# First loads of a one-core decoder step: norm's vector joined to x, one x block issued by ScalarE, the first weight half rounded in two pieces

## The chip, the cores and the metric

The kernel runs on one core of one Trainium2 chip. The metric is the device time of one execution in microseconds (us), as the median of several runs. Engines are named as the profile names them: PE (TensorE matmul), PEld (its weight load), DVE (VectorE), ACT (ScalarE), POOL (GpSimd), SP (SyncE, which here only issues transfers). A name with a q behind it (SPq, ACTq) is the sequencer of that engine, where issuing a transfer takes its time.

## What is computed

One layer of a decoder trunk for 256 prompt tokens and 8 times 4 sample tokens, 288 in all, with a model width of 2048:

```python
xn = rmsnorm(x, norm_mix_g)
proj = jnp.einsum('bld,de->ble', xn, w_in)            # 2048 -> 4096, eight strips of 512
a_val, a_gate, p, c_h, c_b, c_c, d_u, d_v = jnp.split(proj, N_PROJ, axis=-1)
...                                                   # four token mixers A, B, C, D
x = x + jnp.einsum('ble,ed->bld', mix, w_out)
...
xn = rmsnorm(x, norm_ffn_g)
h = jax.nn.silu(jnp.einsum('bld,df->blf', xn, w_gate)) * jnp.einsum('bld,df->blf', xn, w_up)
x = x + jnp.einsum('blf,fd->bld', h, w_down)          # d_ff = 5632
```

A last rmsnorm closes it. All is float32. For this change only the first line and the first strip of the second matter: x times norm's vector `norm_mix_g`, as the moving operand of the products with `w_in`. The factor of the root of the mean square is applied behind the product.

## The kernel before

**Layout.** x lies transposed in `x_sb`: 128 partitions are 128 of the 2048 model columns, and 16 blocks (`KD`) of 288 columns (`T`, the tokens) stand side by side. `X[:, b, :]` is block b. The vectors of the norms and mixers lie in `vec`, with `norm_mix_g` in its first 16 columns (`v(name, b)` is one column).

**Products in three parts.** Every float32 product is made from three products of rounded operands. ScalarE rounds a weight tile `raw` to `wh` (high part), VectorE makes `wl` = `raw` - `wh` (low part); x is treated the same way to `xh_sb` and `xl_sb`, with norm's vector as the scale of the conversion. PE adds wh*xh, wh*xl and wl*xh in the same bank.

**Tiles.** A weight tile is two blocks of 128 rows by 512 columns, 512 KB, in a ring of 4 slots. PE meets 4 column groups of 128 per block, so 12 products of 128x288 per block and 24 per tile. The first two tiles (`HALF_TILES`) are loaded, rounded and used in halves of one block each, by `load_half`, `hi_half`, `lo_half` and `by_kind`; tiles 2 to 5 go whole but still by kind (all 8 wh*xh products, then 8 wh*xl, then 8 wl*xh), and from tile 6 on `products` does the three kinds for each column group in turn.

**Order of the work.** It is written out by hand for each engine; semaphores order the engines among each other. At the start SP issues, one behind the other, x block 0, half 0 of tile 0, x block 1, half 1 of tile 0, x blocks 2 and 3, the two halves of tile 1, x blocks 4 and 5, tile 2 and so on (L364 to L377). From tile 4 on it waits for a slot of the ring. ScalarE issues the first 16 columns of `vec` itself (L458), loads its function table, and then converts and rounds in the order of the tiles: block 0, half 0, block 1, half 1, blocks 2 and 3, the halves of tile 1, blocks 4 and 5, tile 2. VectorE follows it. PE first runs 9 warm-up products (`WARM`, L1247) on a constant, then `by_kind`, whose three groups wait for the x block and the weight half, for the low part of x, and for the low part of the half. The semaphores at the start are `vec_landed`, `x0_landed` (block 0), `first_landed[0]` (half 0 of tile 0), `x_landed[0]` (block 1), `raw_landed[0]` (half 1), and `first_hi`, `first_lo`, `hi_ready`, `lo_ready`, `x_hi`, `x_lo` for what is rounded.

Of the kernel before, what the change touches and what calls it, by code (L numbers as in the profile page):

```python
# [26 lines left out]
P = 128  # L27
D = 2048
KD = D // P
# [3 lines left out]
GRP = 512  # L33
# [57 lines left out]

VECS = [("norm_mix_g", KD), ("conv_a_b", NG), ("ln_a_g", NG), ("ln_a_b", NG), ("pool_scale", NG),
        ("sgu_ln_g", NG), ("sgu_ln_b", NG), ("out_norm_g", KD), ("norm_ffn_g", KD), ("final_norm_g", KD),
# [54 lines left out]
def hybrid_step(nc, a, o):  # L148
    ctx = ExitStack()
    with ctx:  # L150
        def sb(name, cols, dt=F32):
            return ctx.enter_context(nc.sbuf_tensor(name, [P, cols], dt))
# [4 lines left out]
        def blocks(t, n=NG):  # L157
            return t.rearrange("p (n t) -> p n t", n=n)


        x_sb = sb("x_sb", KD * T)
        xh_sb, xl_sb = sb("xh_sb", KD * T, F32R), sb("xl_sb", KD * T, F32R)
        mh_sb, ml_sb = sb("mh_sb", KD * T, F32R), sb("ml_sb", KD * T, F32R)
        raw = sb("raw", RING * TILE)
        wh, wl = sb("wh", RING * TILE, F32R), sb("wl", RING * TILE, F32R)
        X = blocks(x_sb[:, :], KD)
        XH, XL = blocks(xh_sb[:, :], KD), blocks(xl_sb[:, :], KD)
# [41 lines left out]
        def v(name, b):  # L209
            return vec[:, VROW[name] + b:VROW[name] + b + 1]  # L210

        def tap(k, b):
# [45 lines left out]
        def gained(bs):  # L258

            return T0[:, bs.start - 3 * NG:bs.stop - 3 * NG, :] if bs.start >= 3 * NG else GAINED[:, bs, :]  # L260

        Y = x_sb[:, :].rearrange("p (h b t) -> p h b t", h=2, b=KD)
        TOKENS = [slice(h * HT, h * HT + HT) for h in range(2)]
# [6 lines left out]
        x_landed = [sem(f"x_landed{i}") for i in range(XQ)]  # L270
        vec_landed, sgu_landed, mats_landed, hist_landed = (sem(n) for n in (
            "vec_landed", "sgu_landed", "mats_landed", "hist_landed"))
        first_landed = [sem(f"first_landed{t}") for t in range(HALF_TILES)]
# [80 lines left out]
        def _(sp):  # L354
# [8 lines left out]

            sp.dma_start(X[:, 0:1, :], a["x"][:, 0:1, :]).then_inc(x0_landed, 16)  # L364
            load_half(0, 0, first_landed[0])
            sp.dma_start(X[:, 1:2, :], a["x"][:, 1:2, :]).then_inc(x_landed[0], 16)
            load_half(0, 1, raw_landed[0])

            for t in range(1, T_LOOP):
                if t < XQ:  # L370
                    bs = slice(t * TK, (t + 1) * TK)
                    sp.dma_start(X[:, bs, :], a["x"][:, bs, :]).then_inc(x_landed[t], 16)
                if t < HALF_TILES:
                    load_half(t, 0, first_landed[t])
                    load_half(t, 1, raw_landed[t])
                else:
                    load(t, tile_source(t), t - RING + 1 if t >= RING else None, t % RING)  # L377
                if t == XQ:
                    sp.dma_start(vec[:, KD:], a["vec"][:, KD:]).then_inc(hist_landed, 16)
                if t == XQ + 1:  # L380
                    for buf, width, name in ((G, GA, "hist_a"), (PP, PA, "hist_p"), (C, CA, "hist_c")):
                        sp.dma_start(buf[:, :, width:], a[name]).then_inc(hist_landed, 16)
                if t == XQ + 2:
                    sp.dma_start(WT, a["sgu_wt"]).then_inc(sgu_landed, 16)
                if t == XQ + 3:
                    sp.dma_start(PWV, a["pool_w"].rearrange("g c d -> c g d")).then_inc(mats_landed, 16)
                    sp.dma_start(brow[:, :], a["sgu_rows"].to_broadcast([P, NG * P + NG * NS * NS])).then_inc(mats_landed, 16)
# [68 lines left out]
        def _(act):  # L456
            chain = Chain(act, act_chain)
            act.dma_start(vec[:, 0:KD], a["vec"][:, 0:KD]).then_inc(vec_landed, 16)  # L458

# [39 lines left out]
            def x_block(b):  # L499
                act.activation(XH[:, b, :], X[:, b, :], ACT.Copy, scale=v("norm_mix_g", b)).then_inc(x_hi, 1)  # L500

# [5 lines left out]
            def hi_half(t, k):  # L507
                act.wait_ge(*((first_landed[t], 16) if k == 0 else (raw_landed[t], 16)))
                half = slice(k * GRP, (k + 1) * GRP)
                act.activation(slot(wh, t)[:, half], slot(raw, t)[:, half], ACT.Copy).then_inc(first_hi if k == 0 else hi_ready, 1)  # L510

            act.wait_ge(const_ready, 1)
            table(ACT.Copy)
            act.wait_ge(vec_landed, 16)
            act.wait_ge(x0_landed, 16)
            x_block(0)
            hi_half(0, 0)
            act.wait_ge(x_landed[0], 16)
# [177 lines left out]
        def _(dve):  # L696
# [22 lines left out]
            def x_block(b):  # L719
                dve.wait_ge(x_hi, b + 1)  # L720
                dve.scalar_tensor_tensor(out=XL[:, b, :], in0=X[:, b, :], scalar=v("norm_mix_g", b),
                                         in1=XH[:, b, :].bitcast(F32), op0=ALU.mult, op1=ALU.subtract).then_inc(x_lo, 1)
# [131 lines left out]

            dve.wait_ge(vec_landed, 16)
            x_block(0)
# [336 lines left out]
        def _(pe):  # L1193
# [57 lines left out]
            def by_kind(t, ks, hi_made, lo_made):  # L1251
# [3 lines left out]
                pe.wait_ge(x_hi, last_x)  # L1255
                pe.wait_ge(*hi_made)
                for k in ks:
                    for n in range(NG):
                        pe.matmul(bank[n][:, 0:T], W_H[:, k, n * P:(n + 1) * P], XH[:, t * TK + k, :], start=(t == 0 and k == 0), stop=False)  # L1259
                pe.wait_ge(x_lo, last_x)  # L1260
# [155 lines left out]
```

## Time and profile before

| what | value |
|---|---|
| median of three runs | 1177.95 us (1177.62 to 1178.06) |
| the profiled execution's own time | 1178.1 us |
| its span in the trace | 1176.4 us |
| PE busy | 1164.3 us (99%), 8718 products |
| DVE busy | 763.0 us (65%) |
| ACT busy | 502.1 us (43%) |
| POOL busy | 17.6 us (1%) |
| read from memory | 193.00 MB |
| engines of DMA queue q1 (issued by SP) | 54.4% of 16 engines' span |

The span runs from the first instruction to the last of one execution; 1.7 us of the execution lie outside it. Busy times of the engines overlap, and PE's share says which of them has no room. A view by stretches tells where PE is not busy, the timeline of one engine tells what its idle time waited for (in brackets: idle us, and what ended it), and the chain that ended last follows the program back from its end, at each step to what released it.

### The profile page before, as it was taken

Reading aid. Unit: us, or ns where it says so; the run is one execution under the profiler, and the core shown is the slowest. Engines: PE = TensorE matmul, PEld = TensorE weight load, DVE = VectorE, ACT = ScalarE, POOL = GpSimd, SP = SyncE. Lnnn points to the kernel's source line nnn. Section 1 sums busy time; section 2 is a strip of 40 time slices with the busy share of each in tenths; the row PEclk is TensorE's granted clock in tenths of the full one; section 3 lists DMA queues with packets and bytes.
Section 4 is the critical chain, followed back from the end, with each engine's and each line's share of the span. In section 5 each row is a group of like instructions: output and inputs, shape, how many; then the busy total and the mean of one; then the engine's idle time right before and its main releaser. Section 6 shows DMA issues by size and latency. Waiting matters only on the chain.

```text
span 1176.4 us, 22033 instructions
## 1 busy us (share of the span) xinstructions
PE 1164.3 (99%) x8718; PEld 1163.1 (99%) x8718; DVE 763.0 (65%) x1154; ACT 502.1 (43%) x623; POOL 17.6 (1%) x52
## 2 busy tenths in 40 slices
PE   9999999999999999999999999999999999999996
PEld 9999999999999999999999999999999999999996
DVE  6799999987775644744646456455565465645655
ACT  8544545446643333333333343333333333333345
POOL 0000010000000000000000000000000000000003
PEclk9999999999999999999999999999999999999998
DMA  9665545555455555545555555555554555555542
GB/s 313 227 181 171 157 149 170 164 175 161 151 175 172 158 172 161 162 145 191 162 160 163 164 169 164 160 161 165 170 164 143 180 161 170 165 162 161 163 156 84
DMA packets 105385, 197.08 MB, mean 168 GB/s; under 512 B 7936, under 2 KB 11136, under 8 KB 105344
## 3 DMA queue, kind: packets, MB, share of 16 engines
q1 hardware_dynamic: 103088, 195.38, 54.4%
q10 hardware_dynamic: 2256, 1.14, 0.3%
q8 instruction: 28, 0.46, 0.2%
q14 instruction: 13, 0.11, 0.0%
HBM read 193.00 MB, written 3.49 MB: 167 GB/s over the span
## 4 chain that ended last, share of the span: by engine, by line
PE 98%; DVE 0%; DMA 0%; issue 0%; ACT 0%; SPq 0%; DVEq 0%
PE bank L1229 32%; PE bank L1231 32%; PE bank L1230 32%; DMA x_sb<-in_x 0%; PE bank L1259 0%; PE bank L1263 0%; PE bank L1267 0%; DVE x_sb L1176 0%; PE bank L1316 0%; PE bank L1207 0%; ACT xh_sb L500 0%; PE bank L1215 0%; DVEq L150 0%; SPq L362 0%; DVE s_bc L1168 0%
## 5 line engine op out<-in xcount | busy, mean ns | idle before, releaser
L702 DVE TENSOR_TENSOR wl<-raw,wh 128x1024 fp32r<-128x1024 f32 x358 | 435.5, 1222 | 356.1 <-ACT wh L464 355.5
L464 ACT ACTIVATE wh<-raw 128x1024 fp32r<-128x1024 f32 x358 | 379.0, 1061 | 601.0 <-PE bank L1231 595.5
L1229 PE MATMUL bank<-xh_sb,wh 128*128 128x288 f32 x1872 | 554.3, 296 | 0.0
L1230 PE MATMUL bank<-xl_sb,wh 128*128 128x288 f32 x1872 | 552.2, 295 | 0.0
L1231 PE MATMUL bank<-xh_sb,wl 128*128 128x288 f32 x1872 | 550.4, 294 | 0.0
L1231 PEld LDWEIGHTS bank<-xh_sb,wl 128*128 128x128 f32 x1872 | 352.6, 188 | 0.0
L1230 PEld LDWEIGHTS bank<-xl_sb,wh 128*128 128x128 f32 x1872 | 351.5, 188 | 0.0
L1229 PEld LDWEIGHTS bank<-xh_sb,wh 128*128 128x128 f32 x1872 | 350.8, 187 | 0.0
L1229 PE MATMUL bank<-mh_sb,wh 128*128 128x288 f32 x960 | 284.2, 296 | 0.0
L1230 PE MATMUL bank<-ml_sb,wh 128*128 128x288 f32 x960 | 283.2, 295 | 0.0
L1231 PE MATMUL bank<-mh_sb,wl 128*128 128x288 f32 x960 | 282.3, 294 | 0.0
L1231 PEld LDWEIGHTS bank<-mh_sb,wl 128*128 128x128 f32 x960 | 180.8, 188 | 0.0
L1230 PEld LDWEIGHTS bank<-ml_sb,wh 128*128 128x128 f32 x960 | 180.2, 188 | 0.0
L1229 PEld LDWEIGHTS bank<-mh_sb,wh 128*128 128x128 f32 x960 | 179.9, 187 | 0.2 <-issue 0.2
L835 DVE TENSOR_TENSOR x_sb<-bank,x_sb 128x288 f32<-128x288 f32 x207 | 82.0, 448 | 14.7 <-PE bank L1231 14.7
L787 DVE SCALAR_TENSOR_TENSOR work<-g_sb,vec,work 128x256 f32<-128x256 f32 x120 | 52.3, 485 | 0.1
L839 DVE TENSOR_TENSOR p_sb<-bank,g_sb 128x288 f32<-128x288 f32 x44 | 18.9, 453 | 20.2 <-PE bank L1231 20.2
L649 ACT ACTIVATE mh_sb<-p_sb 128x288 fp32r<-128x288 f32 x44 | 18.7, 447 | 17.4 <-DVE p_sb L839 17.4
L843 DVE TENSOR_TENSOR ml_sb<-p_sb,mh_sb 128x288 fp32r<-128x288 f32 x44 | 19.0, 454 | 3.3
L849 DVE TENSOR_TENSOR g_sb<-g_sb,work 128x288 f32<-128x288 f32 x44 | 17.1, 450 | 0.0
L852 DVE TENSOR_TENSOR g_sb<-g_sb,s_bc 128x288 f32<-128x288 f32 x44 | 17.1, 448 | 0.0
L448 POOL TENSOR_TENSOR vt<-work 128x288 f32<-128x288 f32 x1 | 1.2, 1177 | 993.6 <-ACT work L667 993.6
(176 smaller groups left out, 350.3 us busy)
## 6 DMA issues: line engine op xcount, KB each, us to landing
raw<-in_w_gate SPq DMA_DIRECT2D x88, 512.0 KB, 3.7
raw<-in_w_up SPq DMA_DIRECT2D x88, 512.0 KB, 3.6
raw<-in_w_down SPq DMA_DIRECT2D x88, 512.0 KB, 3.8
raw<-in_w_in SPq DMA_DIRECT2D x62, 512.0 KB, 4.3
raw<-in_w_out SPq DMA_DIRECT2D x32, 512.0 KB, 4.0
x_sb<-in_x SPq DMA_DIRECT2D x7, 288.0 KB, 7.2
out_y<-x_sb SPq DMA_DIRECT2D x7, 288.0 KB, 2.2
raw<-in_w_in SPq DMA_DIRECT2D x4, 256.0 KB, 5.0
```

Source lines behind the costliest of these rows:

```text
L464: act.activation(slot(wh, t), slot(raw, t), ACT.Copy).then_inc(hi_ready, 1)
L649: act.activation(MH[:, b, :], HU[:, b, :], ACT.Copy).then_inc(h_hi, 1)
L702: dve.tensor_tensor(slot(wl, t), slot(raw, t), slot(wh, t).bitcast(F32), ALU.subtract).then_inc(lo_ready, 1)
L787: dve.scalar_tensor_tensor(out=acc, in0=src, scalar=tap(k, b), in1=acc, op0=ALU.mult, op1=ALU.add).then_inc(conv_done, 1)
L835: dve.tensor_tensor(X[:, b, :], src[:, 0:T], X[:, b, :], ALU.add).then_inc(banks_free, 1)
L839: dve.tensor_tensor(HU[:, n, :], src[:, 0:T], SG[:, n, :], ALU.mult).then_inc(banks_free, 1)
L843: dve.tensor_tensor(ML[:, b, :], HU[:, b, :], MH[:, b, :].bitcast(F32), ALU.subtract).then_inc(h_lo, 1)
L849: dve.tensor_tensor(SG[:, n, :], SG[:, n, :], T0[:, n, :], ALU.mult).then_inc(ffn_silu, 1)
L852: dve.tensor_tensor(SG[:, n, :], SG[:, n, :], s_bc[:, :], ALU.mult).then_inc(ffn_scaled, 1)
L1229: pe.matmul(banks[n][:, 0:T], W_H[:, k, cols], hi_, start=(first and k == 0), stop=False)
L1230: pe.matmul(banks[n][:, 0:T], W_H[:, k, cols], lo_, start=False, stop=False)
L1231: mm = pe.matmul(banks[n][:, 0:T], W_L[:, k, cols], hi_, start=False, stop=(last and k == TK - 1))
```

## The change

Norm's vector no longer lies in `vec` but in 16 columns in front of x, in memory and in the core (`gx_sb`; `x_sb` is its part behind them). The first transfer brings these 16 columns together with block 0, and the transfer that ScalarE issued for them is gone, with its semaphore `vec_landed`. The transfer of block 1 leaves SP's queue; ScalarE issues it behind its conversion of block 0. The first half of tile 0 is rounded by ScalarE in two pieces of 256 columns, `leading_hi` and `first_hi`; PE waits for the first piece ahead of its first product and for the second ahead of its third.

```diff
-VECS = [("norm_mix_g", KD), ("conv_a_b", NG), ("ln_a_g", NG), ("ln_a_b", NG), ("pool_scale", NG),
+VECS = [("conv_a_b", NG), ("ln_a_g", NG), ("ln_a_b", NG), ("pool_scale", NG),
...
-        x_sb = sb("x_sb", KD * T)
+        gx_sb = sb("x_sb", KD + KD * T)
+        x_sb = gx_sb[:, KD:]
...
+        def mix_gain(b):
+            return gx_sb[:, b:b + 1]
...
-            sp.dma_start(X[:, 0:1, :], a["x"][:, 0:1, :]).then_inc(x0_landed, 16)
+            sp.dma_start(gx_sb[:, 0:KD + T], a["x"][:, 0:KD + T]).then_inc(x0_landed, 16)
             load_half(0, 0, first_landed[0])
-            sp.dma_start(X[:, 1:2, :], a["x"][:, 1:2, :]).then_inc(x_landed[0], 16)
             load_half(0, 1, raw_landed[0])
...
-                    sp.dma_start(vec[:, KD:], a["vec"][:, KD:]).then_inc(hist_landed, 16)
+                    sp.dma_start(vec[:, :], a["vec"]).then_inc(hist_landed, 16)
...
-            act.dma_start(vec[:, 0:KD], a["vec"][:, 0:KD]).then_inc(vec_landed, 16)
...
+            def hi_first_half():
+                act.wait_ge(first_landed[0], 16)
+                for cols, made in ((slice(0, GRP // 2), leading_hi), (slice(GRP // 2, GRP), first_hi)):
+                    act.activation(slot(wh, 0)[:, cols], slot(raw, 0)[:, cols], ACT.Copy).then_inc(made, 1)
+
             act.wait_ge(const_ready, 1)
             table(ACT.Copy)
-            act.wait_ge(vec_landed, 16)
             act.wait_ge(x0_landed, 16)
             x_block(0)
-            hi_half(0, 0)
+            act.dma_start(gx_sb[:, KD + T:KD + 2 * T], a["x"][:, KD + T:KD + 2 * T]).then_inc(x_landed[0], 16)
+            hi_first_half()
...
-                pe.wait_ge(*hi_made)
+                if t == 0 and ks[0] == 0:
+                    pe.wait_ge(leading_hi, 1)
+                else:
+                    pe.wait_ge(*hi_made)
                 for k in ks:
                     for n in range(NG):
+                        if t == 0 and k == 0 and n == NG // 2:
+                            pe.wait_ge(*hi_made)
```

SP's queue at the start of the program, before. `x_sb<-in_x 128x288` is one x block, `128x576` are two, `raw<-in_w_in 128x512` is a weight half:

```order
L364 DMA x_sb<-in_x 128x288
L362 DMA raw<-in_w_in 128x512
L366 DMA x_sb<-in_x 128x288
L362 DMA raw<-in_w_in 128x512
L372 DMA x_sb<-in_x 128x576
L362 DMA raw<-in_w_in 128x512 x2
```

And after, where `128x304` is norm's vector with block 0:

```order
L368 DMA x_sb<-in_x 128x304
L366 DMA raw<-in_w_in 128x512 x2
L375 DMA x_sb<-in_x 128x576
L366 DMA raw<-in_w_in 128x512 x2
L375 DMA x_sb<-in_x 128x576
```

The transfer of block 1 has left the queue between the two halves of tile 0, and everything behind it stands one place further ahead.

ScalarE at the start, before. `xh_sb<-x_sb,vec` is the conversion of an x block, `wh<-raw` the rounding of weights:

```order
L458 DMA vec<-in_vec 128x16
L496 ACT_TABLE_LOAD
L496 ACTIVATE scrap<-ones_d 128x1 [waits const_ready]
L500 ACTIVATE xh_sb<-x_sb,vec 128x288 [waits x0_landed,vec_landed]
L510 ACTIVATE wh<-raw 128x512 [waits first_landed0]
L500 ACTIVATE xh_sb<-x_sb,vec 128x288 [waits x_landed0]
L510 ACTIVATE wh<-raw 128x512 [waits raw_landed0]
```

And after:

```order
L498 ACT_TABLE_LOAD
L498 ACTIVATE scrap<-ones_d 128x1 [waits const_ready]
L502 ACTIVATE xh_sb<-x_sb 128x288 [waits x0_landed]
L523 DMA x_sb<-in_x 128x288
L517 ACTIVATE wh<-raw 128x256 [waits first_landed0]
L517 ACTIVATE wh<-raw 128x256
L502 ACTIVATE xh_sb<-x_sb 128x288 [waits x_landed0]
L512 ACTIVATE wh<-raw 128x512 [waits raw_landed0]
```

A transfer has gone from the head of the queue, another has come between the first conversion and the first rounding, and that rounding is now two instructions.

## Rows read from the trace of the kernel before

**Rows 1.** Stretches: length, busy (count) of five engines, granted clock, DMA share, GB/s.

```profile
5.00:10.00 5.00, 3.72 (x27) 3.31 (x25) 2.92 (x6) 2.82 (x6) 0.00 (x0) 1.00 0.93 304
10.00:14.00 4.00, 4.00 (x30) 4.00 (x31) 3.19 (x6) 3.38 (x7) 0.00 (x0) 1.00 1.05 404
14.00:1165.00 1151.00, 1150.81 (x8636) 1150.41 (x8635) 749.07 (x1129) 489.88 (x599) 15.45 (x20) 1.00 0.55 166
1165.00:1176.40 11.40, 1.79 (x12) 1.56 (x12) 7.22 (x16) 3.33 (x9) 0.00 (x0) 0.67 0.55 208
```

**Rows 2.** Timeline of PE: start, us, engine, line, operation, tiles, count, idle before.

```profile
1.07 4.06 PE L1248 MATMUL bank<-ones_d 128*128 128x128 f32 x18 [1.07 <-POOL ones_d L408]
5.04 0.76 PE L1259 MATMUL bank<-xh_sb,wh 128*128 128x288 f32 x4
...
7.25 0.77 PE L1259 MATMUL bank<-xh_sb,wh 128*128 128x288 f32 x4 [0.40 <-ACT wh L510]
...
9.97 0.77 PE L1259 MATMUL bank<-xh_sb,wh 128*128 128x288 f32 x4 [0.89 <-ACT wh L510]
...
13.23 1.22 PE L1259 MATMUL bank<-xh_sb,wh 128*128 128x288 f32 x8
```

**Rows 3.** Chain that ended last, in order of time: start, us, what.

```profile
2.69 5.63 DMA x_sb<-in_x
8.32 0.02 issue
8.35 0.96 ACT xh_sb L500 x2
9.31 0.53 ACT wh L510
9.84 0.14 issue
```

**Rows 4.** Two transfers by line: x block 0, and tile 1's first half.

```profile
L364 SPq DMA_DIRECT2D x_sb<-in_x x1: 402/402/402, 0.8 to 0.8; - x1
...
DMA to landing us min/median/max: 2.2/2.2/2.2
...
L362 SPq DMA_DIRECT2D raw<-in_w_in x1: 431/431/431, 3.2 to 3.2; - x1
...
DMA to landing us min/median/max: 5.8/5.8/5.8
```

**Rows 5.** Timeline of ScalarE.

```profile
3.24 0.53 ACT L500 ACTIVATE xh_sb<-x_sb,vec 128x288 fp32r<-128x288 f32 x1 [0.47 <-DMA vec<-in_vec]
4.27 0.63 ACT L510 ACTIVATE wh<-raw 128x512 fp32r<-128x512 f32 x1 [0.49 <-DMA raw<-in_w_in]
5.83 0.54 ACT L500 ACTIVATE xh_sb<-x_sb,vec 128x288 fp32r<-128x288 f32 x1 [0.94 <-DMA x_sb<-in_x]
6.48 0.63 ACT L510 ACTIVATE wh<-raw 128x512 fp32r<-128x512 f32 x1
...
11.73 1.06 ACT L464 ACTIVATE wh<-raw 128x1024 fp32r<-128x1024 f32 x1 [0.37 <-DMA raw<-in_w_in]
```

**Rows 6.** Timeline of ScalarE and its sequencer at 61 us.

```profile
61.65 1.06 ACT L464 ACTIVATE wh<-raw 128x1024 fp32r<-128x1024 f32 x1 [2.14 <-PE bank L1231]
61.73 0.64 ACTq L564 DMA_DIRECT2D out_a<-g_sb  x1
```

**Rows 7.** Timeline of SP's sequencer.

```profile
1.74 0.42 SPq L366 DMA_DIRECT2D x_sb<-in_x  x1
...
3.16 0.92 SPq L362 DMA_DIRECT2D raw<-in_w_in  x2
```

**Rows 8.** Stretches of one microsecond each, as in rows 1.

```profile
3.00:4.00 1.00, 1.00 (x7) 1.00 (x6) 0.11 (x1) 0.53 (x1) 0.06 (x2) 1.00 0.85 193
...
5.00:6.00 1.00, 1.00 (x9) 0.99 (x8) 0.62 (x1) 0.17 (x1) 0.00 (x0) 1.00 0.81 235
```

More of the change, by code:

```diff
@@ L165, in hybrid_step @@
         wh, wl = sb("wh", RING * TILE, F32R), sb("wl", RING * TILE, F32R)
-        X = blocks(x_sb[:, :], KD)
+        X = blocks(x_sb, KD)
         XH, XL = blocks(xh_sb[:, :], KD), blocks(xl_sb[:, :], KD)
@@ L260, in gained @@
             return T0[:, bs.start - 3 * NG:bs.stop - 3 * NG, :] if bs.start >= 3 * NG else GAINED[:, bs, :]
-        Y = x_sb[:, :].rearrange("p (h b t) -> p h b t", h=2, b=KD)
+        Y = x_sb.rearrange("p (h b t) -> p h b t", h=2, b=KD)
         TOKENS = [slice(h * HT, h * HT + HT) for h in range(2)]
@@ L270, in hybrid_step @@
         x_landed = [sem(f"x_landed{i}") for i in range(XQ)]
-        vec_landed, sgu_landed, mats_landed, hist_landed = (sem(n) for n in (
-            "vec_landed", "sgu_landed", "mats_landed", "hist_landed"))
+        sgu_landed, mats_landed, hist_landed = (sem(n) for n in ("sgu_landed", "mats_landed", "hist_landed"))
+        leading_hi = sem("leading_hi")
         first_landed = [sem(f"first_landed{t}") for t in range(HALF_TILES)]
@@ L370, in _ @@
                 if t < XQ:
-                    bs = slice(t * TK, (t + 1) * TK)
-                    sp.dma_start(X[:, bs, :], a["x"][:, bs, :]).then_inc(x_landed[t], 16)
+                    at = slice(KD + t * TK * T, KD + (t + 1) * TK * T)
+                    sp.dma_start(gx_sb[:, at], a["x"][:, at]).then_inc(x_landed[t], 16)
                 if t < HALF_TILES:
@@ L499, in x_block @@
             def x_block(b):
-                act.activation(XH[:, b, :], X[:, b, :], ACT.Copy, scale=v("norm_mix_g", b)).then_inc(x_hi, 1)
+                act.activation(XH[:, b, :], X[:, b, :], ACT.Copy, scale=mix_gain(b)).then_inc(x_hi, 1)
             def x_part(q):
@@ L720, in x_block @@
                 dve.wait_ge(x_hi, b + 1)
-                dve.scalar_tensor_tensor(out=XL[:, b, :], in0=X[:, b, :], scalar=v("norm_mix_g", b),
+                dve.scalar_tensor_tensor(out=XL[:, b, :], in0=X[:, b, :], scalar=mix_gain(b),
                                          in1=XH[:, b, :].bitcast(F32), op0=ALU.mult, op1=ALU.subtract).then_inc(x_lo, 1)
@@ L852, in silu @@
                     dve.tensor_tensor(SG[:, n, :], SG[:, n, :], s_bc[:, :], ALU.mult).then_inc(ffn_scaled, 1)
-            dve.wait_ge(vec_landed, 16)
+            dve.wait_ge(x0_landed, 16)
             x_block(0)
@@ L1378 @@
     host = {
-        "x": tokens.reshape(T, KD, P).transpose(2, 1, 0),
+        "x": np.concatenate([rows("norm_mix_g"), tokens.reshape(T, KD, P).transpose(2, 1, 0).reshape(P, KD * T)], axis=1),
         "vec": np.concatenate([rows(name) for name, _ in VECS], axis=1),
```

## The prediction, made before the changed kernel had run

> **What bounds the kernel now.** I read the stretches first, because a change that touches only the first loads can gain only what the first stretch loses. From 14 us to 1165 us the profile has TensorE (PE) busy 1150.81 of 1151.00 us, and 4.00 of 4.00 between 10 and 14 us, at a granted clock of 1.00, the 2.4 GHz level; behind 1165 us stands the closing norm with its stores, 11.40 us, which the change leaves alone [rows 1]. So the end of the program is the start of PE's unbroken run plus a fixed sum, and the reader should look for where that run starts. PE's own timeline gives it: nine warm-up products reach to 5.13 us, the first 12 real products start at 5.04 with no idle time before them, then come 0.40 us of waiting to 7.25 and 0.89 us to 9.97, both for ScalarE's rounding of a weight half (L510); from 9.97 on nothing waits [rows 2]. The chain that ended last says what 9.97 hangs on: the transfer of x blocks 2 and 3, issued at 2.69 and landing at 8.32, two x conversions to 9.31, the weight half 0.53 more to 9.84, and 0.14 of hand-over [rows 3]. That is the only path on which this change can move the end.
>
> **A ceiling comes before any sum.** All that PE idles between its first real product and its unbroken run is 0.40 + 0.89 = 1.29 us [rows 2]. The first product cannot start much before 5.0, since the warm-up holds PE until then. Even with every wait gone the gain is about 1.3 us, 0.11% of 1178 us. A measurement of this kernel tells about 0.2% (2.4 us) from no change, so a measurable gain is out of reach; the question is only which tenth of a microsecond it is, and whether something breaks.
>
> **Part 1, norm's vector in front of x.** It removes ScalarE's own transfer of vec and the wait for it. x block 0 was issued at 0.81 and took 2.2 us to land, so it was there at 3.0 [rows 4]; the first conversion started at 3.24, released by vec [rows 5]. The merged transfer carries 304 columns for 288, 6% more, so 3.0 to 3.05: the first conversion moves forward by about 0.2 us. What is late next is the first weight half: ScalarE idles 0.49 us for it up to 4.27 [rows 5]. The 0.2 us only lengthen that wait. Value 0. If the merged piece landed 0.5 us later, 3.55 + 0.53 = 4.08 would still be ahead of 4.27, so 0 on that side too.
>
> **Part 2, the first weight half rounded in two pieces.** A rounding of 512 columns takes 0.63 us and one of 1024 takes 1.06 [rows 5], so about 0.43 us per 512 columns and 0.2 fixed: a piece of 256 costs 0.40, the pair 0.7 to 0.8 against 0.63. The first piece is ready at 4.27 + 0.40 = 4.67, the second at 4.98 to 5.07. Before, the whole half was ready at 4.90. PE does not take the first piece at 4.67, because its warm-up holds it to about 5.0, where the real products start back to back with it [rows 2]. The products of columns 2 and 3 need the second piece 0.26 us after the first product, at 5.3, and get it by 5.1. So +0.05 us of gain at most and no loss at the start; and since PE then waits for block 1 and its weight half anyway (the 0.40 us to 7.25), it is swallowed. VectorE's subtraction of this half starts 0.1 to 0.2 us later, ahead of its use after eight products. Value 0.
>
> **Part 3, block 1 moved from SP's queue to ScalarE's.** Three things hang on it.
> First, ScalarE's own time. Its queue issues the transfer behind the first conversion. In this trace an issue on that queue began at 61.73, 0.08 us after an ACTIVATE of 1.06 us had started [rows 6], so the two overlap: the issue runs from about 3.1 to 3.7. Were it not to overlap, 3.03 + 0.53 + 0.64 = 4.20 is still before 4.27. Value 0 either way.
> Second, block 1 is issued at 3.1 for 1.74 before. The lower bound of its flight is the 2.2 us of a transfer into empty queues [rows 4], so 5.3; the upper one the 5.63 us that blocks 2 and 3 took in SP's queue [rows 3], so 8.7; between them stands its own old flight, 1.74 to 5.83, 4.1 us [rows 5, 7], so 7.2. I take 6.0 to 6.5, near the lower end, since ScalarE's queue holds nothing else while SP's holds four transfers. What it may cost: ScalarE needs 0.54 + 0.63 us and a gap of 0.11, 1.28 from 5.83 to 7.11 [rows 5], and is then free for blocks 2 and 3, which are awaited to 8.32. Block 1 may land as late as 8.32 - 1.28 = 7.04 before it delays them. At 6.5 PE's first wait grows by 0.6 us, and its second shrinks by as much. Value 0 at 6.5, and at 8.7 a loss of 1.7.
> Third, all that SP issues behind it comes 0.47 us earlier (the spacing from 2.69 to 3.16 [rows 3, 7]): blocks 2 and 3 at 2.21, tile 1's halves, blocks 4 and 5, tile 2. If flight times stay, all land 0.47 earlier. If the 16 DMA engines are what paces them, they land when they did, because the bytes up to there are the same with block 1 in them. The rows stand between. From 3 to 4 us the engines are busy 0.85 of the time at 193 GB/s, from 5 to 6 0.81 at 235 [rows 8], against 1.05 at 404 from 10 to 14 [rows 1]: not full, but near it. I take half of it, 0.25 us.
>
> A rule stands against this part. The Trainium skill ("DMA: Bandwidth & Descriptors", section "Issuing engines are not separate DMA queues") says that transfers started from several engines run on the same 16 DMA engines and interleave, and that this saves only issue time. By it the sum would be 0 instead of 0.25; it is the first rival.
>
> **What caps the gain behind it.** With blocks 2 and 3 early, the next things are late. Tile 1's first half, issued at 3.16 and 5.8 us in flight, lands at 8.96 [rows 4, 7]; with 0.53 and 0.14 behind it PE could start at 9.65, 0.32 earlier, if it does not move. Tile 2 landed at 11.73, where ScalarE waited 0.37 us for it, and is rounded at 12.79 [rows 5]; PE takes it up at 13.23 [rows 2], which leaves 0.3 us after a hand-over of 0.14. These two say that 0.3 is the limit unless the whole stream comes forward, and 0.25 lies under it.
>
> **Sum.** 0 + 0 + 0 + 0.25 = 0.25 us off. Against the profiled execution: 1178.1 - 0.25 = 1177.85. That execution lies 0.15 us over the median, so the time to be expected as a median is 1177.95 - 0.25 = 1177.7. The vec transfer that SP issues later keeps its 208 columns and its place; x_sb grows by 16 columns and vec shrinks by 16, and no steady instruction changes shape.
>
> **Rivals.**
> No movement: the engines pace the early stream, blocks 2 and 3 land at 8.32 as before. For it speaks that the old flights grow along the queue (2.2, 4.1, 5.63, 5.8 us); against it the unfilled 15 to 19% between 3 and 6 us. Time 1177.95. Chance 0.27.
> The stream comes forward whole: the 0.47 us carry through to tile 2, and PE's run starts at 9.5: 1177.95 - 0.47 = 1177.5, and 1176.65 if all 1.29 us went. Against it: ScalarE is free for blocks 2 and 3 only from about 7.1, and then needs 0.96 + 0.53 + 0.14, so 8.7 is the floor. Chance 0.15.
> Slower, by one mechanism: block 1 comes late on its new queue. The mechanism decides at a landing of 7.04; every 0.1 us past that costs 0.1, because conversion, rounding and blocks 2 and 3 stand behind it on ScalarE. With the old flight of 4.1 us it lands at 7.2 and costs 0.2; with 5.63 it costs 1.7, 1179.6. I price it at 0.5: 1178.45. Chance 0.12.
> Slower rows: with 16 columns in front, each partition's row of x starts elsewhere in memory, and its reads may be less efficient. If the x rows went at the 304 GB/s of 5 to 10 us where they could have 404 [rows 1], a transfer of 288 KB would take 0.97 us for 0.73, and two such lie ahead of 8.32: up to 0.48 us, 1178.4. Against it: nothing in the rows says that the start of a row matters. Chance 0.04.
> The Trainium skill ("DMA: Bandwidth & Descriptors", "How a descriptor splits into AXI transactions") says that a read that does not start on a 256-byte boundary fetches unused bytes; the new rows start 64 bytes on, which would make some beats per row more and a loss of under 0.1 us. No run shows it so far.
> The forecast itself (a gain between 0.1 and 0.4 us) has 0.42.
>
> **How the numbers follow.** Likeliest 1177.7. The three runs of before spread over 1177.62 to 1178.06, so 0.2 either way comes on top of each case. The range reaches from the stream that comes forward whole (1177.5 less 0.4) to the late block 1 at its price: 1177.1 to 1178.45. Faster by over 0.2% would need 2.4 us, above the ceiling of 1.29: 0.01. Slower by over 0.2% needs block 1 to land at 9.4, above the upper bound of 8.7: 0.02. Within 0.2%: 0.97.
>
> **What would show it.** Right: the last transfer on the chain is still an early one, PE's run starts between 9.6 and 9.9, the first conversion at about 3.05, the first real product still at 5.0, the issue on ScalarE's queue over before 4.2, block 1 there by 7.0. Part 2 is wrong if the first product starts before 4.9 or PE waits between its columns 1 and 2. Part 3 is wrong if the first wait of PE grows past 7.9. All of it is wrong if PE idles anywhere behind 10 us, or if the steady products change their pace: of the 8636 between 14 and 1165 us [rows 1] one nanosecond each is 8.6 us.

## The result, and the profile after

The changed kernel takes 1181.79 us (median of seven executions, 1179.21 to 1182.99), against 1177.63 us (1177.45 to 1178.06) for the kernel before, measured beside it: a ratio of 1.0033, with a 95% interval of 1.0024 to 1.0043. It is 4.2 us slower. The range had ended at 1178.45, and the chance given to a loss of over 0.2% was 0.02.

The profiled execution is the mildest of the seven, 1179.21 us, with a span of 1177.5 us against 1176.4. It shows the first part of the loss whole. PE's timeline (start, us, engine, line, operation, tiles, count, idle time before), to be held against [rows 2]:

```profile
4.89 0.78 PE L1271 MATMUL bank<-xh_sb,wh 128*128 128x288 f32 x4
...
6.03 0.69 PE L1279 MATMUL bank<-xh_sb,wl 128*128 128x288 f32 x4
9.41 0.78 PE L1271 MATMUL bank<-xh_sb,wh 128*128 128x288 f32 x4 [2.69 <-ACT wh L512]
...
14.27 1.22 PE L1271 MATMUL bank<-xh_sb,wh 128*128 128x288 f32 x8
```

The first group starts 0.15 us earlier, and then PE waits 2.69 us where it had waited 0.40. The second wait (0.89 us) is gone. The last row is the first product of tile 2, which stood at 13.23 [rows 2]. It is the best single reading of this case: from there on PE never stops, so its shift of 1.04 us is the shift of the end (1177.5 for 1176.4, 1.1 us). ScalarE's timeline and its sequencer, against [rows 5], say why:

```profile
3.10 0.54 ACT L502 ACTIVATE xh_sb<-x_sb 128x288 fp32r<-128x288 f32 x1 [0.80 <-DMA x_sb<-in_x]
3.10 0.42 ACTq L523 DMA_DIRECT2D x_sb<-in_x  x1
...
4.12 0.72 ACT L517 ACTIVATE wh<-raw 128x256 fp32r<-128x256 f32 x2 [0.48 <-DMA raw<-in_w_in]
...
8.21 0.54 ACT L502 ACTIVATE xh_sb<-x_sb 128x288 fp32r<-128x288 f32 x1 [3.37 <-DMA x_sb<-in_x]
8.65 0.61 ACT L512 ACTIVATE wh<-raw 128x512 fp32r<-128x512 f32 x1
```

The small edits came out as worked: the first conversion at 3.10, the issue of block 1 overlapping it and over at 3.52, the two pieces taking 0.72 us. Then ScalarE sits idle 3.37 us for block 1. The view of its line gives the flight, the time from the start of the issue to the landing:

```profile
L523 ACTq DMA_DIRECT2D x_sb<-in_x x1: 424/424/424, 3.1 to 3.1; - x1
...
DMA to landing us min/median/max: 5.1/5.1/5.1
```

The chain that ended last now names this transfer, where it had named the one of blocks 2 and 3 [rows 3]:

```profile
3.10 5.08 DMA x_sb<-in_x
8.19 0.02 issue
8.21 0.54 ACT xh_sb L502
8.74 0.53 ACT wh L512
9.27 0.14 issue
```

From 9.41 on PE is the chain itself. So far that is 1.1 us. The other six executions took 1181.47 us and more. What they have besides stands in the first experiment.

### The profile page after: what moved, and what is told of

It reads as the page before. It is cut to its first block, busy times and chain, and to the rows that moved or that the text cites. A ratio compares the mean times of both kernels' runs of the same rounds, so it can differ in the third digit from the quotient of the medians.

```text
span 1177.5 us, 22032 instructions
## 1 busy us (share of the span) xinstructions
PE 1163.9 (99%) x8718; PEld 1163.1 (99%) x8718; DVE 762.8 (65%) x1154; ACT 501.9 (43%) x624; POOL 18.5 (2%) x52
## 4 chain that ended last, share of the span: by engine, by line
PE 98%; DMA 1%; DVE 0%; issue 0%; ACT 0%; DVEq 0%
PE bank L1236 32%; PE bank L1238 32%; PE bank L1237 32%; DMA x_sb<-in_x 1%; PE bank L1271 1%; PE bank L1275 0%; PE bank L1279 0%; DVE x_sb L1183 0%; PE bank L1328 0%; PE bank L1214 0%; PE bank L1222 0%; DVEq L150 0%; DVE s_bc L1175 0%; ACT xh_sb L502 0%; PE bank L1308 0%
```

## The experiments

The theory behind them (one): block 1, issued late, lands behind what has been issued before it, whichever queue it is on, and PE's long wait for it then takes the granted clock down. Its rivals: the shifted x rows load slower; ScalarE's queue is slow in itself; the pieces of the first half do harm. "Theory two" in an expectation is the rival that this experiment sets against theory one, and not always the same. All medians stand beside the kernel before on the same chip.

**The changed kernel again** (no edit).

> The changed kernel again, for more executions of it. Theory one (block 1 lands late from ScalarE's queue, PE idles about 2.7 us, and in most executions the granted clock falls in or behind that gap): again about 1181.8 as a median against 1177.6, with a spread of some 2 us, and a profile that has either the 2.69 us wait at clock 1.00 (time near 1179.2) or the same or a longer wait and a stretch at half clock (time 1181 to 1183). Theory two (x rows that start 64 bytes on load slower): the same median, but then the wait would be for all x transfers, with their flights longer than before.

Measured 1181.68 us (1180.79 to 1182.23) against 1177.66, ratio 1.0032 (1.0020 to 1.0044). This time the profiled execution (1181.76 us, span 1180.0) is a typical one. PE's timeline:

```profile
10.44 0.77 PE L1271 MATMUL bank<-xh_sb,wh 128*128 128x288 f32 x4 [3.72 <-ACT wh L512]
...
12.45 1.16 PE L1271 MATMUL bank<-xh_sb,wh 128*128 128x288 f32 x4
13.41 1.16 PE L1275 MATMUL bank<-xl_sb,wh 128*128 128x288 f32 x4
...
16.83 1.22 PE L1271 MATMUL bank<-xh_sb,wh 128*128 128x288 f32 x8
```

and the stretches (length, busy and count of PE, PEld, DVE, ACT, POOL, granted clock, DMA share, GB/s):

```profile
10.00:11.00 1.00, 0.56 (x4) 0.59 (x5) 1.00 (x3) 1.00 (x3) 0.00 (x0) 1.00 1.04 402
11.00:12.00 1.00, 1.00 (x9) 1.00 (x8) 1.00 (x4) 1.00 (x3) 0.00 (x0) 0.84 1.05 409
12.00:13.00 1.00, 1.00 (x6) 1.00 (x6) 1.00 (x2) 1.00 (x4) 0.00 (x0) 0.50 1.10 351
...
14.00:15.00 1.00, 1.00 (x6) 1.00 (x5) 0.98 (x1) 1.00 (x3) 0.00 (x0) 0.50 1.00 379
```

where the mild execution has

```profile
12.00:13.00 1.00, 1.00 (x10) 1.00 (x9) 0.91 (x3) 1.00 (x3) 0.00 (x0) 1.00 1.06 396
```

Two things differ from the mild execution. Block 1 landed at 9.2 us (its flight took 6.0 us for 5.1), so PE waited 3.72 us. And the granted clock fell to 0.50, the 1.2 GHz level, shortly after PE had taken up work again: four products take 0.96 us from start to start (12.45 to 13.41) where they take 0.53. From the start of the second group to that of tile 2 this execution needs 16.83 - 10.44 = 6.39 us, the mild one 14.27 - 9.41 = 4.86 for the same 36 products: 1.53 us of clock. The whole shift is 16.83 - 13.23 = 3.6 us, that of the span 3.6 too: 2.1 from the late block, 1.5 from the clock. (By the medians the loss is 4.0 us; the profile of the kernel before is of an execution that took 1178.1 us, 0.4 over the median here.)

**Part 1 alone**: norm's vector in front of x. The changed kernel with

```diff
             load_half(0, 0, first_landed[0])
+            sp.dma_start(gx_sb[:, KD + T:KD + 2 * T], a["x"][:, KD + T:KD + 2 * T]).then_inc(x_landed[0], 16)
             load_half(0, 1, raw_landed[0])
...
-            act.dma_start(gx_sb[:, KD + T:KD + 2 * T], a["x"][:, KD + T:KD + 2 * T]).then_inc(x_landed[0], 16)
-            hi_first_half()
+            hi_half(0, 0)
...
```

and with PE's two waits for the pieces put back to the one wait of before.

> Norm's vector in front of x alone; block 1 stays in SP's queue behind tile 0's first half, no split. Theory one: no loss, 1177.4 to 1177.9. Theory two (the shifted rows are what costs): the loss of the whole change is here, 1179 to 1182.

Measured 1177.90 us (1177.39 to 1178.39), ratio 1.0001 (0.9992 to 1.0010). The shifted rows cost nothing that can be measured. That rival falls.

**Part 3 alone**: the kernel before with

```diff
-            sp.dma_start(X[:, 1:2, :], a["x"][:, 1:2, :]).then_inc(x_landed[0], 16)
...
             x_block(0)
+            act.dma_start(X[:, 1:2, :], a["x"][:, 1:2, :]).then_inc(x_landed[0], 16)
             hi_half(0, 0)
```

> The kernel before with block 1's transfer issued by ScalarE behind its first conversion and nothing else changed; the rows of x start where they did. Theory one: the whole loss, 1181 to 1182.5, block 1 landing at 8 us or later, PE's wait about 2.7 us or more. Theory two: no loss, 1177.6.

Measured 1181.89 us (1181.31 to 1182.86), ratio 1.0035 (1.0022 to 1.0049): the whole loss. Its profiled execution was a long one (1182.70 us, span 1181.0), with a flight of 5.8 us, a wait of 3.01 us and tile 2 at 17.83, 4.6 us late:

```profile
10.32 1.30 PE L1259 MATMUL bank<-xh_sb,wh 128*128 128x288 f32 x4 [3.01 <-ACT wh L509]
...
17.83 1.22 PE L1259 MATMUL bank<-xh_sb,wh 128*128 128x288 f32 x8
```

**Part 2 alone, and parts 1 and 2 together.** The kernel before with the pieces `leading_hi` and `first_hi`; and the changed kernel with block 1 back in SP's queue as above, the pieces kept.

> The kernel before with the first weight half rounded in two pieces and nothing else. Theory one: nothing, 1177.5 to 1177.9, first real product at 5.0 us or up to 0.15 earlier, PE's run from 9.97 on as before. Rival: the earlier end of the first group lengthens the wait behind it and by that costs clock: 1178.5 or more.

> The changed kernel with block 1 back in SP's queue behind tile 0's first half: parts 1 and 2 of the change without part 3. Theory one (part 3 is all of the loss): 1177.3 to 1178.0, no difference from before. Rival (the parts add up to something that neither has alone): 1178.5 or more.

Measured 1177.42 us (1177.23 to 1178.24), ratio 0.9999 (0.9990 to 1.0008), and 1177.73 us (1177.26 to 1178.21), ratio 1.0001 (0.9992 to 1.0010). Neither does anything that can be measured. Part 3 is the whole of the case.

**The same transfer at the same moment from SP's queue.** The changed kernel, block 1 issued by SP between the two halves of tile 1:

```diff
                 if t < HALF_TILES:
                     load_half(t, 0, first_landed[t])
+                    sp.dma_start(gx_sb[:, KD + T:KD + 2 * T], a["x"][:, KD + T:KD + 2 * T]).then_inc(x_landed[0], 16)
                     load_half(t, 1, raw_landed[t])
...
-            act.dma_start(gx_sb[:, KD + T:KD + 2 * T], a["x"][:, KD + T:KD + 2 * T]).then_inc(x_landed[0], 16)
```

> The changed kernel, but block 1 is issued by SP, at the moment at which ScalarE issued it (3.1 us), behind blocks 2 and 3 and tile 1's first half. Theory one: lands at 8 to 9 us as from ScalarE's queue, PE waits 2.5 to 3.7 us, time 1181 to 1182.5. Theory two (ScalarE's queue is the culprit): lands earlier, by 7, time under 1179.

Measured 1180.74 us (1179.23 to 1181.06), ratio 1.0023 (1.0014 to 1.0033). That is 3.0 us over the kernel before, where the changed kernel run again was 4.0 over it on another chip (the two intervals overlap). SP's sequencer and ScalarE:

```profile
3.15 0.43 SPq L378 DMA_DIRECT2D x_sb<-in_x  x1
...
7.90 0.53 ACT L503 ACTIVATE xh_sb<-x_sb 128x288 fp32r<-128x288 f32 x1 [2.78 <-DMA x_sb<-in_x]
```

A flight of 4.7 us. Some three quarters of the loss (3.0 of 4.0 us) are there without ScalarE's queue; a rest remains that theory one does not explain: from ScalarE's queue the flights were 5.1, 6.0, 5.8 and, below, 6.2 us. The order is not quite the same either: SP issues tile 1's second half at 3.63 here, behind block 1, and at 3.16 in the changed kernel. Of the 2.25 us by which tile 2 starts later, 1.52 are the clock, which fell here too (6.38 us from the second group to tile 2 for 4.86), and the other 0.73 the late landing. What was expected of theory one was missed on three counts, each by little: the time by a quarter of a microsecond, the landing (7.9 for 8 to 9 us) and PE's wait (2.00 for 2.5 to 3.7). The time lies between the two expectations, nearer to that of theory one.

**The same transfer at the head of ScalarE's queue.** The line moved to the top of ScalarE's program, ahead of its table load.

> The changed kernel, but ScalarE issues block 1 as its first instruction, at 0.8 us, ahead of its table load. Theory one (a transfer lands behind what has been issued before it, on whichever queue): block 1 lands at 3.5 to 4.5 us, PE's wait between the first two groups is gone or under 0.5 us, no half clock, and the time is 1176.5 to 1177.6, at or below the kernel before. Theory two (ScalarE's queue is slow in itself beside SP's): flight of 5 us again, landing at 5.8 or later, time about as before, 1177.6 to 1178.5.

Measured 1177.16 us (1176.85 to 1177.67) against 1177.77, ratio 0.9995 (0.9986 to 1.0004). The same queue, the same transfer, 2.3 us earlier: its view gives

```profile
L461 ACTq DMA_DIRECT2D x_sb<-in_x x1: 418/418/418, 0.8 to 0.8; - x1
...
DMA to landing us min/median/max: 3.3/3.3/3.3
```

so it lands at 4.1, PE's first wait is gone, and tile 2 starts at 12.64, 0.6 us before [rows 2]. Block 0, issued by SP at the same 0.81, pays for it: its conversion starts at 3.91 for 3.10. Theory two in its plain form (a slow queue) falls.

**Behind the table load.** The line between `table(ACT.Copy)` and the wait for block 0.

> The changed kernel, but ScalarE issues block 1 behind its table load, at 2.1 us, ahead of its wait for block 0: between the head (0.8 us, landed at 4.1) and the changed kernel (3.1 us, landed at 8.2 to 9.2). If the landing follows what has been issued before it: 5.5 to 7 us, PE's wait 0.5 to 1.5 us, time 1177.3 to 1178.3. If ScalarE's queue starts late beside a filled SP queue, whatever the moment: 7.5 or later, 1179 or more.

Measured 1177.22 us (1176.62 to 1177.46) against 1177.57, ratio 0.9996 (0.9987 to 1.0005). The point between was missed, for a reason worth seeing:

```profile
0.81 1.28 ACT L498 ACT_TABLE_LOAD   x1 [0.81 <-PEq L1405]
1.05 0.40 ACTq L521 DMA_DIRECT2D x_sb<-in_x  x1
...
6.75 0.77 PE L1271 MATMUL bank<-xh_sb,wh 128*128 128x288 f32 x4
...
11.64 1.30 PE L1271 MATMUL bank<-xh_sb,wh 128*128 128x288 f32 x8
```

The sequencer issued at 1.05, while the table was still loading, and not behind it at 2.1. The flight was 2.6 us, PE ran from 5.00 without a wait, and tile 2 stood at 11.64, 1.6 us early (span 1174.9). But this is one of the fastest of the eleven executions (1176.65 us). Over all of them the median gain is 0.35 us, inside the interval of no change.

**One transfer for norm's vector and blocks 0 and 1**, SP's first.

> The changed kernel, but norm's vector, block 0 and block 1 come as one transfer, SP's first. Theory one: as issued at the head, with one transfer less: it lands at 3.6 to 4.1 us, PE's first two groups run without a gap, 1176.8 to 1177.5. Rival: the larger first transfer delays the first weight half and blocks 2 and 3 by as much as it brings block 1 forward: 1177.6 to 1178.2.

Measured 1177.42 us (1176.68 to 1178.58), ratio 0.9998 (0.9989 to 1.0007). It landed at 4.0, block 1 thus 1.8 us earlier than in the kernel before; the two weight halves came 0.4 and 0.3 us later (4.7 and 6.7 us for 4.3 and 6.4). The median lies in the range of theory one, but the interval holds the rival's too.

**SP holds the stream back** until block 0 is converted:

```diff
             load_half(0, 1, raw_landed[0])
+            sp.wait_ge(x_hi, 1)
```

> The changed kernel, but SP holds everything behind tile 0's second half until block 0 is converted (3.7 us), so that block 1 meets only the two weight halves. Theory one: block 1 lands at 5.5 to 6.5 us though issued at 3.1 from ScalarE's queue, PE's first wait is under 1 us; the stream behind comes 1.5 us later, so PE waits again behind it, for 1 to 2 us, with no half clock: 1178 to 1179.5. Theory two: block 1 still takes 5 us and lands past 8, time 1181 or more.

Measured 1178.26 us (1177.85 to 1178.73), ratio 1.0004 (0.9995 to 1.0013). Block 1 is issued by ScalarE at 3.2 as in the changed kernel, and lands at 6.8:

```profile
3.22 0.40 ACTq L524 DMA_DIRECT2D x_sb<-in_x  x1
...
6.84 0.53 ACT L503 ACTIVATE xh_sb<-x_sb 128x288 fp32r<-128x288 f32 x1 [1.85 <-DMA x_sb<-in_x]
```

A flight of 3.6 us, 1.5 to 2.6 less, with blocks 2 and 3 and tile 1's halves taken out of its way. That the backlog (what has been issued and has not landed) sets the landing is shown from both sides: by an earlier issue and by a shorter backlog at the same moment. It landed 0.3 us later than expected, and PE's first wait was 1.07 us; the second wait, expected at 1 to 2 us, did not come: blocks 2 and 3, issued at 3.77, were there at 7.0, in time for ScalarE.

**Nothing issued behind it.** SP waits for block 1 ahead of tile 1's second half, `sp.wait_ge(x_landed[0], 16)`.

> The changed kernel, but SP issues nothing further until block 1 has landed, so that only what was issued before it (two transfers of x, three weight halves) can be ahead of it; looked at for the flight of block 1 alone, the time is worse in any case. If the later SP transfers slip in ahead of it and make the flight of 6 us from ScalarE's queue against 4.7 from SP's: a flight of 4 to 4.8 us. If a transfer on ScalarE's queue starts late beside a filled SP queue whatever comes behind it: 5.5 to 6.5 us.

Measured 1179.61 us (1179.13 to 1182.55), ratio 1.0018 (1.0008 to 1.0029), a flight of 5.0 us. That lies between the two expectations and settles little: nearer to SP's 4.7 than to the 5.8 to 6.2 of three other profiles, but the mildest execution of the changed kernel had 5.1 with everything behind it. Its profile (1180.89 us) has the clock at 0.50 too, behind a wait of 2.78 us. And it limits the word backlog:

```profile
7.00:8.00 1.00, 0.00 (x0) 0.00 (x0) 0.00 (x0) 0.00 (x0) 0.00 (x0) 1.00 0.19 71
```

Between 7 and 8 us the DMA engines were busy 0.19 of the time, and still block 1 was not there. So the end of its wait was not that all 16 engines were busy with other transfers.

**Block 1's packets, in the traces of the runs above.** The profile counts the packets of each queue in a stretch. ScalarE's queue is q10: where SP issues block 1, q10 has no packet from 3 to 10 us, and in the changed kernel it has 144, 0.15 MB, which is block 1. The mild execution, which issued it at 3.10, from 4 to 5, 5 to 6 and 6 to 7 us (packets, MB, share of 16 engines):

```profile
q1 hardware_dynamic: 140, 0.28, 97.2%
...
q1 hardware_dynamic: 182, 0.34, 89.6%
q10 hardware_dynamic: 15, 0.02, 6.6%
...
q1 hardware_dynamic: 105, 0.19, 54.7%
q10 hardware_dynamic: 86, 0.09, 38.1%
```

Its first packet moved between 5.5 and 5.75 us, 2.4 us or more after the issue, with the engines busy for SP's queue until then; with SP held back the first moved between 4.25 and 4.5, 1.0 to 1.3 us after the issue. The landings have an order as well. In all seven profiles in which block 1 was issued between 3.0 and 3.4 us, it landed behind every x or weight transfer issued before it and ahead of every one issued after it, whichever queue they were on. The mild execution issued it at 3.10, ahead of tile 1's second half (3.16), and it landed first, at 8.2 for 9.0; the changed kernel run again issued it at 3.21, behind that half, and it landed behind it, at 9.2 for 8.6. That is theory one, seen directly.

**The changed kernel with PE's gap filled.** Ten more warm-up products behind the first group:

```diff
                 by_kind(t, (0,), (first_hi, t + 1), (first_lo, t + 1))
+                if t == 0:
+                    for _ in range(BRIDGE):
+                        pe.matmul(bank[BANKS + 1][:, 0:P], ones_d[:, :], ones_d[:, :], start=True, stop=True)
```

> The changed kernel with ten more warm-up products on PE behind its first 12 real ones (about 2.1 us at full clock), which fill the wait for block 1. Block 1 lands as late as before. If the clock is the second part of the loss: no half clock, PE's second group at 9.4 to 10.4 us, time 1178.6 to 1179.8. If the lateness alone made the 4 us: 1181 to 1182 again.

Measured 1180.19 us (1179.38 to 1180.77), ratio 1.0020 (1.0011 to 1.0029): 2.4 us over the kernel before, where the changed kernel was 4.0 over it. That is 0.4 us over what was expected of the clock and 0.8 under what was expected without it. PE's timeline and one stretch:

```profile
7.48 2.39 PE L1287 MATMUL bank<-ones_d 128*128 128x128 f32 x20
10.43 0.77 PE L1272 MATMUL bank<-xh_sb,wh 128*128 128x288 f32 x4 [0.55 <-ACT wh L513]
...
15.28 1.22 PE L1272 MATMUL bank<-xh_sb,wh 128*128 128x288 f32 x8
```

```profile
12.00:14.00 2.00, 2.00 (x17) 2.00 (x17) 1.94 (x4) 2.00 (x5) 0.00 (x0) 1.00 1.01 345
```

The granted clock stays at 1.00, and from the second group to tile 2 PE needs 15.28 - 10.43 = 4.85 us, as in the mild execution of the changed kernel. This is with block 1 as late as in the changed kernel run again: a flight of 6.2 us, a landing at 9.2. What is left, 2.4 us by the medians, is the lateness; the 1.5 us from the second group to tile 2 that the filler saved are the clock. The second group started at 10.43, at the end of the expected 9.4 to 10.4; that the time is above its range all the same comes from the profile of the kernel before, which is of an execution (1178.1 us) 0.3 us over the median here.

**The long gap alone, on the kernel before.** No transfer moves; PE's second group waits until a later x block is converted than it needs, as if block 1 had come late:

```diff
-                last_x = t * TK + ks[-1] + 1
+                last_x = 4 if t == 0 and ks[0] == 1 else t * TK + ks[-1] + 1
```

> The kernel before, with its transfers and conversions untouched; only PE's second group waits for block 3's conversion too, so PE idles from 6.9 to about 9.4 us and runs unbroken from there. Its lateness is 9.4 + 1.6 - 9.97 = 1.0 us. If an idle PE is what costs clock: a stretch of half clock behind the gap in most executions, 1.7 us more, 1180.2 to 1180.8. If the clock fell for a reason of the transfers: 1178.5 to 1179.0.

Measured 1178.91 us (1178.15 to 1180.62), ratio 1.0013 (1.0004 to 1.0022). Of eleven executions three took 1180.13 to 1180.62 us and eight 1178.15 to 1179.38. "Most executions" was wrong: the median lies in the range of the other theory. The profiled execution was the mildest; its blocks 2 and 3 had landed so early, and its first group ended so late, that PE's gap was only 0.68 us:

```profile
8.36 0.79 PE L1259 MATMUL bank<-xh_sb,wh 128*128 128x288 f32 x4 [0.68 <-ACT xh_sb L500]
```

In this execution the kernel did not make the gap that it was meant to make, and the others have no profile; it settles nothing. The next two make the gap longer.

**A longer gap**: the same with 6 in the place of 4.

> As idle_only (transfers and conversions of the kernel before), but PE's second group waits for block 5's conversion, to about 11.4 us. Its lateness is 11.5 + 1.6 - 9.97 = 3.1 us, 1180.7. If an idle PE is what costs clock, a stretch of half clock stands behind the gap in all or nearly all executions and adds 1.7 us or more: 1182.4 to 1184.2. If it is not, 1180.7 to 1181.2.

Measured 1183.27 us (1182.14 to 1183.95) against 1177.57, ratio 1.0044 (1.0030 to 1.0058), in the range expected if an idle PE costs clock.

**The longer gap, filled**: the same again, with 16 warm-up products in the gap, as above.

> As idle_longer, with 16 warm-up products in PE's gap (some 3.8 us). The same lateness, but PE is not idle: if idleness is what costs clock, no half clock and 1180.5 to 1181.3, about 2 us under idle_longer. If not, as idle_longer.

Measured 1180.76 us (1180.36 to 1181.34), ratio 1.0025 (1.0015 to 1.0035), again as expected. The two kernels differ by these 16 products alone, and the one that does more work is 2.5 us faster; the slowest of its nine executions (1181.34) lies under the fastest of the other's five (1182.14). PE and a stretch of the unfilled one:

```profile
11.45 1.33 PE L1259 MATMUL bank<-xh_sb,wh 128*128 128x288 f32 x4 [4.55 <-ACT xh_sb L500]
12.58 1.16 PE L1263 MATMUL bank<-xl_sb,wh 128*128 128x288 f32 x4
...
19.07 1.09 PE L1259 MATMUL bank<-xh_sb,wh 128*128 128x288 f32 x7
```

```profile
12.00:14.00 2.00, 2.00 (x10) 2.00 (x9) 1.18 (x2) 1.80 (x4) 0.00 (x0) 0.50 1.05 402
```

and of the filled one:

```profile
6.74 3.73 PE L1275 MATMUL bank<-ones_d 128*128 128x128 f32 x32
11.41 0.79 PE L1260 MATMUL bank<-xh_sb,wh 128*128 128x288 f32 x4 [0.94 <-ACT xh_sb L501]
```

```profile
12.00:14.00 2.00, 2.00 (x16) 1.92 (x15) 1.19 (x3) 1.80 (x4) 0.00 (x0) 1.00 1.06 407
```

The second group starts at the same moment in both (11.45 and 11.41). DMA share and GB/s of the stretch are alike, PE is busy through the whole of it in both, and its clock is 0.50 in one and 1.00 in the other. Tile 2 starts at 19.07 in the one and at 16.43 in the other. No transfer stands where the changed kernel has it. What takes the clock here is that PE idles.

## Why the prediction was wrong, step by step

**What held.** Part 1 and part 2 were priced at 0, and measured at 1.0001 and 0.9999, both together at 1.0001. The first conversion was forecast at 3.05 and stood at 3.10, the issue on ScalarE's queue overlapped it as in [rows 6], the pair of pieces took 0.72 us (forecast 0.7 to 0.8), and PE took its first product at 4.89. (That is 0.15 us earlier and not 0.05, and just past the sign "before 4.9" by which part 2 was to be wrong; behind it PE waits anyway, so it was worth nothing.) The rival of slower rows, and with it the rule on AXI transactions named beside it, shows nothing that can be measured here. The rows do not all start 64 bytes on, by the way: the step from one partition's row to the next grew as well, from 18432 to 18496 bytes, so each row starts elsewhere.

The frame held too: the end of the program is the start of PE's unbroken run plus a fixed sum. In every profile the span moved by what tile 2's first product moved, to 0.1 us. The product moved by +1.0 (after), +3.6 (the changed kernel again), +4.6 (part 3 alone), +2.3 (from SP's queue), +2.1 (filled), -0.6 (at the head), +5.8 (longer gap).

**The stream did come forward**, and by more than the 0.25 us of the sum. In the mild profile the view of the line of blocks 2 and 3 and then that of tile 1's first half end in

```profile
DMA to landing us min/median/max: 4.8/4.8/4.8
...
DMA to landing us min/median/max: 4.9/4.9/4.9
```

Issued at 2.21 and 2.69, they were there at 7.0 and 7.6, where they had come at 8.32 [rows 3] and 8.96 [rows 4]: 1.3 us earlier. Some of that is the spread of single executions. Over all profiles, the blocks 2 and 3 landed at 7.3 to 8.4 us in the seven whose SP queue has the old order (median 7.9), and at 6.7 to 7.4 in the six with block 1 issued at 3.1 to 3.3 us and SP not held back (median 7.0): about 0.9 us. Block 1, issued behind them, no longer lay before them. But nothing takes them: ScalarE converts in block order, and stands before block 1 until 8.21. The gain was real and lay off the path.

**The first step that failed** is the flight of block 1: "I take 6.0 to 6.5, near the lower end, since ScalarE's queue holds nothing else while SP's holds four transfers." From ScalarE's queue with the stream running, the landings were 8.2 to 9.2, so the flights 5.1 to 6.2 us, where 2.9 to 3.4 had been taken: 1.7 to 3.3 us more, and on both sides of the upper bound of 5.63. An empty queue is no empty path. The rows that should have had the weight are those of transfers issued at the same moment: 5.63 us for the one at 2.69 [rows 3], 5.8 for the one at 3.16 [rows 4]. The flight goes by the backlog: 2.6 us issued at 1.05 and 3.3 at 0.8 (one profile each; these two alone are out of order), 3.6 at 3.2 with SP held back, 4.7 at 3.2 from SP's queue with the stream running. The Trainium skill's rule ("DMA: Bandwidth & Descriptors", section "Issuing engines are not separate DMA queues") was weighed against a gain of 0.25 us only. It bears far more on this step: if another engine's queue is no separate path, a later issue is a later landing. The landings of the seven profiles agree: they keep the order of issue across both queues.

**The second step that failed** is a term that was missing. "Every 0.1 us past that costs 0.1" held as far as it went: a landing at 8.19 makes 8.19 - 7.04 = 1.15 us, and the mild execution lost 1.1; one at 9.2 makes 2.2, and the changed kernel run again lost 2.1 without its clock. That it fits so well is luck. The 7.04 was worked out for the path over ScalarE and blocks 2 and 3; the path that decided is block 1's own over PE: 0.02 + 0.54 + 0.53 + 0.14 us from the landing to the second group, and 1.68 us of its twelve products, 8.19 + 2.91 = 11.10 for the 11.09 at which tile 1 starts, with its first half rounded by 10.7. That path decides from 9.97 - 2.91 = 7.06 on, by chance nearly the same. But a wait of 3.7 us in PE also costs the clock, 1.5 us in that execution and 2.6 between the two kernels of the longer gap. With the landing and the clock the sum is 2.1 + 1.5 = 3.6 us, and the span was 3.6 longer. The text held the means to see this: it read the granted clock as 1.00 and asked only how much of PE's idle time could go, never what a new idle stretch would do to the clock. That also made the bound for "slower by over 0.2%" wrong: 2.4 us were thought to need a landing at 9.4, and come with one at 9.2 and less. The Trainium skill ("TensorE: Matmul & The Clock Gate", section "What's actually happening") says that the slow clock is the default state and activity what lifts it; the filled kernels agree, at 1.00 for 0.50.

**The rival that came nearest** was "slower, by one mechanism: block 1 comes late on its new queue". It had the place and, by that luck, the point from which it decides. Its size was wrong by both steps above, and its chance, 0.12, was far too low. It was also priced at 0.5 us, though its own upper bound gave 1.7 and 1179.6: the range ended at 1178.45 for that reason, and even the mild execution's 1179.21 lies past it. Besides the one on the first product, two of the signs of being wrong came true: PE's second group started past 7.9 (at 9.41), and in the changed kernel run again PE idled behind 10 us. "No movement" and "the stream comes forward whole" fell.

**Still open.** From ScalarE's queue block 1 flew 5.1 to 6.2 us, from SP's 4.7 at the same moment in the one profile there is. Up to 1 us of the 4.2 may hang on that; the kernel with nothing issued behind it (5.0 us) didn't settle it. Part of it lies in the stream: in the six profiles in which SP was not held back, tile 1's first half, issued ahead of block 1, landed anywhere from 7.3 to 8.3 us, and block 1 landed 0.1 to 0.9 us behind the transfer issued just before it, from SP's queue 0.4. Why the last packets take so long with the engines mostly idle (the kernel with nothing behind) is open as well. Nor is it settled when the clock falls: the mild execution idled 2.69 us and kept it, that from SP's queue idled 2.00 us and lost it, as its rows show:

```profile
9.10 1.30 PE L1271 MATMUL bank<-xh_sb,wh 128*128 128x288 f32 x4 [2.00 <-ACT wh L513]
10.20 1.16 PE L1275 MATMUL bank<-xl_sb,wh 128*128 128x288 f32 x4
...
12.83 0.69 PE L1275 MATMUL bank<-xl_sb,wh 128*128 128x288 f32 x4
```

## What to carry to other kernels

A transfer on another engine's queue is not an early one: take its flight from the transfers issued at the same moment, whatever their queue, and issue what is needed first, first. A new wait of PE is priced by its length and by the clock that PE may lose in it, so look at both before trading a short wait for a chance of a longer one. If such a gap can't be avoided, a few products into a spare bank keep the clock; here ten of them saved 1.5 us and sixteen 2.5. Neither kernel got back to the time of the kernel before.

## What the runs showed of the hardware

ScalarE's sequencer started a DMA issue 0.24 us into a table load (1.05 against 0.81), and at 3.10 together with an ACTIVATE: an issue put behind an instruction in the text need not wait for its end. After a long gap PE did not always run at the slow clock at once. In the changed kernel run again the second group started at 10.44 with 0.77 us for four products, and only 1.2 us later the clock stood at 0.50, with four products each 0.96 us instead of 0.53; with nothing issued behind block 1 it was 1.4 us. In three other profiles (part 3 alone, from SP's queue, the longer gap) the clock had fallen by the time PE took up work, and the first four products took 1.30 to 1.33 us. A granted clock of 1.00 in the first microseconds is not the whole story either: with part 3 alone it is 1.00 from 5 to 6 us, and the first four products take 1.17 us, where the kernel before has 0.76; why, no run shows. Landings kept the order of issue across two queues in the seven profiles named above. Executions of one kernel differed here by up to 3.8 us (1179.21 to 1182.99); the two that have a profile differ by 2.5, of which 1.0 is the landing of one early transfer and 1.5 the clock.
